# Decoding the 16 chosen routes in one 128x512 pass instead of two 128x256 passes, in an f32 two-block network on one core

## The chip, the cores and the metric

One core of one Trainium2 chip runs the whole program in one launch. The metric is the device time in microseconds (us); lower is better. The kernel before was timed in three runs, and one further execution of it was profiled.

## What is computed

The inputs are f32. A first block (norm, four mixers, projection, MLP) works on 256 tokens of width 1024. A second block has two layers over 272 tokens (16 meta tokens and the 256). Each layer ends in a product-key lookup of experts, `peer`, and that is where the change lies. Cut to it:

```python
PEER_HEADS, PEER_N_KEYS, PEER_TOPK = 8, 128, 16
def peer(h, w_query, sub_keys, u, v):          # u, v: (128 * 128, 1024) per layer
    q = einsum('btd,dq->btq', hx, w_query).reshape(B, T, 8, 2, 128)
    s = einsum('bthpc,hpnc->bthpn', q, sub_keys)            # 128 scores in each of 2 halves
    top_s, top_i = lax.top_k(s, 16)
    cand_s = (top_s[..., 0, :, None] + top_s[..., 1, None, :])      # 256 sums
    cand_i = (top_i[..., 0, :, None] * 128 + top_i[..., 1, None, :])
    best_s, best_pos = lax.top_k(cand_s, 16)
    expert = jnp.take_along_axis(cand_i, best_pos, axis=-1)
    gate = jax.nn.softmax(best_s, axis=-1)
    act = gelu(einsum('btd,bthkd->bthk', hx, u[expert]))
    return einsum('bthk,bthkd->btd', gate * act, v[expert])
```

So each token picks 8 x 16 experts, and for each of them a row of `u` and a row of `v` (4 KB each) is read from HBM.

## The kernel before, in words

The pairs of token and head are worked off in 33 **units** (`UNITS`) of 128 partitions: 32 tokens by 4 heads, and one unit with the 16 meta tokens by 8 heads. Seventeen units belong to layer 0 and sixteen to layer 1. Two neighbouring units share a group of 32 tokens. A unit has 16 **slots**, one per chosen expert; slot k needs one gathered 128x1024 f32 tile (512 KB) of `u` and one of `v`.

Five queues share the work, each strictly in the order in which the program was written:

- **GpSimd** (`peer_gpsimd`, L496 to L518) issues 528 gathers of `u` and 528 of `v`, both at L505, in turn: `u` of slot i, then `v` of slot i-22. Before a gather it waits until its ring buffer is free (7 buffers for `u`, freed by the dot product; 6 for `v`, freed by TensorE), and before the first `u` gather of a unit until VectorE has written that unit's expert numbers (`experts_ready`).
- **VectorE** (`peer_vector`, L602 to L625) takes the slots of unit s in four quarters. A quarter is four dot products of a gathered `u` tile with the token rows, which lie in PSUM (L568); then, in the first quarter, the weights of the unit before (`weights_of`, L577 to L585), in the second, the addition of a finished group to the residual (`add_group`, L598); then one of the four **stages of a route** for unit s+2 (`route`, L438 to L483). Some routes around the change of layer are placed by a table (`LATE`, L485), two stages at once.
- **TensorE** (`peer_tensor`, L642) multiplies the weights with the `v` tiles (L551) and lays the token rows of the next group into PSUM (`unit_rows`, L531 and L534). In between it computes the queries, and the attention and projections of layer 1 (L691, L760 to L787).
- **ScalarE** copies scores out of PSUM (L372) and computes exponentials and gelu (L633, L640).
- **SyncE** loads the dense weights (L1572) and stores the output.

The route of a unit, in stages: stages 0 and 1 find the top 16 of the 128 scores of either half (L449 to L453); stage 2 adds them to 256 sums and finds their top 16 (L461 to L465, then L449 to L453 again); **stage 3 is the decode**. It turns the 16 positions, each 0 to 255, into expert numbers: high and low four bits (L471, L472), made float (L473); then for either half a 16x16 one-hot matrix by comparison with 0..15 (L476), times the half's 16 indices (L478), summed along each row (L479); and last the two sums added into `expert` (L482), which signals `experts_ready`. `done` puts a drain behind each instruction of this sequence (L446). Two routes are worked before the first slot (L606 to L608); the other 31 lie in the loop.

Under L476 to L479, `w0`, `w1` and `w2` are the three 128x256 parts of the tile `work`: `w0` and `w1` hold the one-hot matrices of the two halves.

Of the kernel before, what the change touches and what calls it, by code (L numbers as in the profile page):

```python
# [8 lines left out]
ALU = mybir.AluOpType  # L9
ACT = mybir.ActivationFunctionType  # L10
X = mybir.AxisListType.X

P = 128
# [16 lines left out]
PH, KEYS, TOPK = 8, 128, 16  # L30
# [23 lines left out]
def program(nc, x, pre_mix_g, w_in, conf_dw_w, conf_dw_b, conf_gn_g, conf_gn_b, sconv_w, lru_conv_w,  # L54
# [4 lines left out]
    with ctx:  # L59
        def sb(name, shape, dt=F32):  # L60
            return ctx.enter_context(nc.sbuf_tensor(name, shape, dt))
# [3 lines left out]
        def S(name):  # L65

            if name not in named:
                named[name] = nc.alloc_semaphore(name=name)
                count[name] = 0
            return named[name]  # L70
# [39 lines left out]
        work = sb("work", [P, 3, 256])  # L110
# [3 lines left out]
        half_f = sb("half_f", [P, 2, TOPK])  # L114
        best = sb("best", [P, DEEP, TOPK])
        best_at = sb("best_at", [P, TOPK], U32)
        pos_f = sb("pos_f", [P, 2, TOPK])
        picked = sb("picked", [P, 2, TOPK])
# [6 lines left out]
        iota16 = sb("iota16", [P, TOPK])  # L125
# [164 lines left out]
        def slots_done(engine, name, n):  # L290

            layer = 0 if n <= SPLIT else 1
            engine.wait_ge(S(f"{name}{layer}"), n - SPLIT * layer)
# [132 lines left out]
        def score_slot(u):  # L426

            return u if u < L0_UNITS else 9 + (u - L0_UNITS) % 8

        def scores_ready(dve, u):  # L430

            if u < L0_UNITS:
                dve.wait_ge(S("ffn0_scores_out"), SCORE_ORDER.index(u) + 1)
            else:
                _, t, _, half = UNITS[u]
                dve.wait_ge(S("f_scores_out"), 2 * t + half + 1)

        def route(dve, u, stage):  # L438

            v = nc.vector  # L440
            at = u % DEEP
            w0, w1, w2 = (work[:, i, :] for i in range(3))
            square = [P, TOPK, TOPK]

            def done(instruction):
                dve.drain()  # L446

            def top16(values, index, source, rest):
                done(v.max(values[:, 0:8], source))  # L449
                done(v.max_index(index[:, 0:8], values[:, 0:8], source))  # L450
                done(v.match_replace(rest, values[:, 0:8], source, MASKED))
                done(v.max(values[:, 8:16], rest))  # L452
                done(v.max_index(index[:, 8:16], values[:, 8:16], rest))  # L453

            if stage < 2:
                if stage == 0:
                    scores_ready(dve, u)
                part = slice(P * stage, P * (stage + 1))
                top16(half_v[:, stage, :], half_i[:, stage, :], scores[:, score_slot(u), part], w1[:, part])
            if stage == 2:  # L460
                v.tensor_scalar(half_f[:, 0, :], half_i[:, 0, :], float(KEYS), float(UNITS[u][0] * EXPERTS),  # L461
                                ALU.mult, ALU.add)
                v.tensor_copy(half_f[:, 1, :], half_i[:, 1, :])
                sums = w2.rearrange("p (i j) -> p i j", i=TOPK)
                done(v.tensor_tensor(sums, half_v[:, 0, :].unsqueeze(2).broadcast_to(square),  # L465
                                     half_v[:, 1, :].unsqueeze(1).broadcast_to(square), ALU.add))
                top16(best[:, at, :], best_at[:], w2, w0)
            if stage == 3:
                v.tensor_scalar(neg_best[:, at:at + 1], best[:, at, 0:1], -1.0, None, ALU.mult)\
                    .then_inc(S("best_ready"), 1)  # L470
                v.tensor_scalar(ints[:, 0, :], best_at[:].bitcast(I32), 4, None, ALU.logical_shift_right)  # L471
                done(v.tensor_scalar(ints[:, 1, :], best_at[:].bitcast(I32), TOPK - 1, None, ALU.bitwise_and))  # L472
                done(v.tensor_copy(pos_f[:], ints[:]))  # L473
                for p, w in enumerate((w0, w1)):
                    onehot = w.rearrange("p (i j) -> p i j", i=TOPK)
                    done(v.tensor_tensor(onehot, pos_f[:, p, :].unsqueeze(2).broadcast_to(square),  # L476
                                         iota16[:].unsqueeze(1).broadcast_to(square), ALU.is_equal))
                    done(v.tensor_tensor(onehot, onehot, half_f[:, p, :].unsqueeze(1).broadcast_to(square), ALU.mult))  # L478
                    done(v.tensor_reduce(picked[:, p, :], onehot, X, ALU.add))  # L479
                if u >= DEEP:  # L480
                    slots_done(dve, "v_used", TOPK * (u - DEEP + 1))
                done(v.tensor_tensor(expert[:, at, :], picked[:, 0, :], picked[:, 1, :], ALU.add)  # L482
                     .then_inc(S("experts_ready"), 1))  # L483
# [5 lines left out]
        def routes_at(dve, s, j):  # L489

            late = {u for u, _ in LATE.values()}
            u, stages = LATE.get((s, j), (s + 2, (j,) if s + 2 < len(UNITS) and s + 2 not in late else ()))
            for stage in stages:
                route(dve, u, stage)
# [107 lines left out]
        def peer_vector(dve):  # L602

            v = nc.vector
            units = len(UNITS)
            for u in range(2):  # L606
                for stage in range(4):
                    route(dve, u, stage)  # L608
            for s in range(units):
                for j in range(4):  # L610
                    dots_of(dve, s, range(4 * j, 4 * j + 4))
                    if j == 0 and s >= 1:
                        weights_of(dve, s - 1)
                    if j == 1 and s >= 2 and closes_group(s - 2):
                        add_group(dve, s - 2)
                    routes_at(dve, s, j)
                    if (s, j) == (PH - 2, 3):
                        dve.wait_ge(S("ffn0_scores_done"), L0_UNITS)
                        v.tensor_copy(meta_spread.rearrange("p k (h t) -> p k h t", h=PH),
                                      hnt[:, :, 0:META].unsqueeze(2).broadcast_to([P, KD, PH, META]))\  # L620
                            .then_inc(S("meta_spread"), 1)
                    for t in range(NT):
                        attend_dve(dve, t, 4 * s + j - ATTEND[t])
            weights_of(dve, units - 1)
            add_group(dve, units - 1)  # L625
# [1061 lines left out]
```

## Time and profile before

| what | value |
|---|---|
| three timed runs, median (lowest to highest) | 2005.23 us (2003.51 to 2007.88) |
| the profiled execution, its own time | 2004.27 us |
| span of that execution in the profile | 2002.5 us |
| PE busy | 1477.6 us (74%) |
| VectorE (DVE) busy | 1187.2 us (59%) |
| GpSimd (POOL) busy | 1025.1 us (51%) |
| ScalarE (ACT) busy | 279.0 us (14%) |
| moved by DMA | 669.93 MB |

The span runs from the first to the last instruction of the profiled execution; its own time is 1.8 us longer. Busy time counts an engine's instructions, not its waits. The gathers run from 458.6 us of the span to its end; what comes before is the first block, the pooling layer and the first queries.

### The profile page before, as it was taken

How to read it: one execution, taken by the hardware profiler on the slowest of the kernel's cores; microseconds unless marked ns; L12 is line 12 of the kernel's file. 1: busy time of each engine (PE TensorE's matmuls, PEld its weight loads, DVE VectorE, ACT ScalarE, POOL GpSimd, SP SyncE). 2: the span in 40 equal slices, each digit the busy share in tenths (PEclk: the TensorE clock that was granted, in tenths of full speed). 3: DMA queues.
4: the chain of work that ended last, by engine and by line, in shares of the span. 5: the costliest groups of instructions: out<-in, count | busy, mean ns of one | idle time of the engine just before them, and what ended most of it. 6: DMA issues, size and time to landing. Idle time of an engine off the chain costs nothing.

```text
span 2002.5 us, 19164 instructions
## 1 busy us (share of the span) xinstructions
PE 1477.6 (74%) x6422; PEld 588.6 (29%) x6422; DVE 1187.2 (59%) x2799; ACT 279.0 (14%) x539; POOL 1025.1 (51%) x1099
## 2 busy tenths in 40 slices
PE   6979999784667556668888885687797866656666
PEld 5736666474233110102223222022232210101100
DVE  3641000258787756787669636976786587777752
ACT  2141111211001100001212111012321110010000
POOL 2000000004777766676556655774565677677675
PEclk9988999887688866768996998689988976677668
DMA  9113346106999999999999999999989999999998
GB/s 330 62 75 137 132 162 266 59 22 216 381 409 409 409 409 410 406 409 384 409 403 346 410 409 387 410 408 409 397 325 409 410 410 409 399 410 409 397 400 328
DMA packets 189387, 669.93 MB, mean 335 GB/s; under 512 B 19806, under 2 KB 20960, under 8 KB 188016
## 3 DMA queue, kind: packets, MB, share of 16 engines
q0 software_dynamic: 152064, 553.72, 70.4%
q1 hardware_dynamic: 37232, 115.09, 15.1%
q8 instruction: 46, 0.75, 0.2%
q14 instruction: 45, 0.37, 0.0%
HBM read 667.68 MB, written 1.05 MB: 334 GB/s over the span
## 4 chain that ended last, share of the span: by engine, by line
DMA 30%; POOL 14%; PE 14%; DVE 13%; issue 7%; DVEq 2%; ACT 1%; POOLq 0%; ACTq 0%
DMA big<-in_peer_v,expert 21%; POOL big L505 14%; DMA big<-in_peer_u,expert 9%; DVE big L568 8%; PE ps L551 4%; PE ps L691 3%; PE ps L534 2%; PE ps L334 2%; DVEq L446 2%; PE ps L785 1%; DVE residual L598 0%; PE ps L787 0%; PE ps L1657 0%; DVE half_v L452 0%; DVE diag L585 0%
## 5 line engine op out<-in xcount | busy, mean ns | idle before, releaser
L551 PE MATMUL ps<-big,diag 128*32 128x512 f32 (+1 forms) x2112 | 710.4, 792 | 438.8 <-DMA big<-in_peer_v,expert 403.1
L568 DVE CUSTOM_DVE_ANT_0 big<-big,ps 128x1024 f32<-128x1024 f32 x528 | 625.4, 1218 | 332.4 <-DMA big<-in_peer_u,expert 229.4
L505 POOL DMA_INDIRECT big<-in_peer_u,expert x528 | 501.6, 950 | 319.2 <-issue 133.8
L505 POOL DMA_INDIRECT big<-in_peer_v,expert x528 | 506.8, 960 | 249.3 <-PE ps L551 132.5
L551 PEld LDWEIGHTS ps<-big,diag 128*32 128x32 f32 (+1 forms) x2112 | 83.5, 121 | 972.3 <-DMA big<-in_peer_v,expert 848.0
L691 PE MATMUL ps<-big 128*128 128x512 f32 x384 | 195.4, 632 | 1.0 <-ACT big L880 1.0
L1585 POOL MEMSET big<- 128x128 f32 x3 | 0.5, 202 | 373.9 <-POOLq L1449 373.9
L230 DVE RECIPROCAL stats<-stats 128x1 f32<-128x1 f32 (+1 forms) x17 | 2.8, 162 | 252.0 <-ACT stats L224 251.5
L1505 PE MATMUL ps<-ua,big 128*128 128x256 f32 x512 | 116.3, 382 | 0.0
L1516 PE MATMUL ps<-big,sc 128*128 128x512 f32 x256 | 114.4, 592 | 0.0
L1505 PEld LDWEIGHTS ps<-ua,big 128*128 128x128 f32 x512 | 98.3, 192 | 25.4 <-issue 13.2
L691 PEld LDWEIGHTS ps<-big 128*128 128x128 f32 x384 | 66.9, 194 | 127.8 <-issue 125.9
L640 ACT ACTIVATE dots<-dots 128x16 f32<-128x16 f32 x33 | 7.1, 216 | 593.3 <-DVE dots L568 593.2
L334 PEld LDWEIGHTS ps<-big 128*128 128x128 f32 x512 | 71.1, 217 | 16.9 <-issue 15.8
L334 PE MATMUL ps<-big 128*128 128x144 f32 (+1 forms) x512 | 74.8, 311 | 0.8 <-DVE big L317 0.8
L1374 PE MATMUL ps<-sc,big 128*128 128x256 f32 x288 | 64.2, 385 | 3.5 <-DVE sc L1234 3.5
L598 DVE TENSOR_TENSOR residual<-residual,ps 32x512 f32<-32x512 f32 (+1 forms) x68 | 46.5, 683 | 31.2 <-PE ps L551 28.8
L1516 PEld LDWEIGHTS ps<-big,sc 128*128 128x128 f32 x256 | 48.6, 190 | 49.3 <-issue 47.8
L1374 PEld LDWEIGHTS ps<-sc,big 128*128 128x128 f32 x288 | 55.4, 193 | 11.9 <-DVE sc L1234 3.7
L534 PE MATMUL ps<-ident,big 128*32 128x128 f32 x1024 | 56.0, 341 | 0.0
L534 PEld LDWEIGHTS ps<-ident,big 128*32 128x32 f32 x1024 | 44.7, 134 | 13.8 <-issue 10.6
L640 ACT ACT_TABLE_LOAD x33 | 42.3, 1283 | 28.8 <-DVE dots L568 28.4
(293 smaller groups left out, 1201.6 us busy)
## 6 DMA issues: line engine op xcount, KB each, us to landing
big<-in_mlp_w SPq DMA_DIRECT2D x16, 2048.0 KB, 7.8
big<-in_w_kv SPq DMA_DIRECT2D x32, 512.0 KB, 6.9
big<-in_peer_wq SPq DMA_DIRECT2D x32, 512.0 KB, 6.8
big<-in_w_in SPq DMA_DIRECT2D x5, 2048.0 KB, 17.6
big<-in_peer_u,expert POOLq DMA_INDIRECT x528, 10.3
big<-in_peer_v,expert POOLq DMA_INDIRECT x528, 10.3
big<-in_peer_wq SPq DMA_DIRECT2D x1, 8192.0 KB, 27.2
big<-in_w_q SPq DMA_DIRECT2D x16, 512.0 KB, 6.9
```

The costliest lines, as they stand in the source:

```text
L334: last = nc.tensor.matmul(bank(4 + hp % 2)[:, 0:cols], wq_peer[:, k, P * hp:P * (hp + 1)], hnt[:, k, at:at + cols], start=(k == 0), stop=( ...
L446: dve.drain()
L505: nc.gpsimd.indirect_dma_start(out=ring[n % len(ring)], out_offset=None, in_=rows[name], in_offset=bass.IndirectOffsetOnAxis(ap=expert[:, ...
L534: last = nc.tensor.matmul(to[TOK * j:TOK * (j + 1), :], hnt[:, k, at:at + TOK], ident[:], start=True, stop=True)
L551: last = nc.tensor.matmul(acc[r:r + tokens, :], placed(u, tokens)[:, k, :], ring_v[n % len(ring_v)][:, BANK * half:BANK * (half + 1)], sta ...
L568: nc.vector.tensor_tensor_reduce(out=slot, in0=slot, in1=rows_x, scale=1.0, scalar=0.0, op0=ALU.mult, op1=ALU.add, accum_out=dots[:, u % 2 ...
L598: last = v.tensor_tensor(to, to, bank(group % 2)[r:r + tokens, :], ALU.add)
L640: a.activation(dots[:, s % 2, :], dots[:, s % 2, :], ACT.Gelu).then_inc(S("gelu_done"), 1)
L691: last = m.matmul(bank(b + half), src, w[:, BANK * half:BANK * (half + 1)], start=(k == 0), stop=(k == KD - 1))
L1374: last = m.matmul(bank(b)[:, T * c:T * (c + 1)], win[chunk][:, k, P * (at + c):P * (at + c + 1)], ht[:, k, :], start=(k == 0), stop=(k == ...
L1505: last = m.matmul(bank(4 + q % FT)[:, 0:T], w1b[b][:, k, P * (q % FT):P * (q % FT + 1)], h2t[:, k, :], start=(k == 0), stop=(k == KD - 1))
L1516: last = m.matmul(bank(2 * t + half), act2[:, q % FT, P * t:P * (t + 1)], w2b[b][:, q % FT, BANK * half:BANK * (half + 1)], start=False, s ...
```

## The change

Stage 3 of a route no longer loops over the two halves. `work[:, 0:2, :]`, 512 contiguous columns that hold both one-hot matrices, is seen as 32 rows of 16, and each of the three operations works on all of it at once.

```diff
-                for p, w in enumerate((w0, w1)):
-                    onehot = w.rearrange("p (i j) -> p i j", i=TOPK)
-                    done(v.tensor_tensor(onehot, pos_f[:, p, :].unsqueeze(2).broadcast_to(square),
-                                         iota16[:].unsqueeze(1).broadcast_to(square), ALU.is_equal))
-                    done(v.tensor_tensor(onehot, onehot, half_f[:, p, :].unsqueeze(1).broadcast_to(square), ALU.mult))
-                    done(v.tensor_reduce(picked[:, p, :], onehot, X, ALU.add))
+                both = [P, 2 * TOPK, TOPK]
+                flat = work[:, 0:2, :].rearrange("p w (i j) -> p (w i) j", i=TOPK)
+                halves = work[:, 0:2, :].rearrange("p w (i j) -> p w i j", i=TOPK)
+                done(v.tensor_tensor(flat, pos_f[:, :, :].rearrange("p w i -> p (w i)").unsqueeze(2).broadcast_to(both),
+                                     iota16[:].unsqueeze(1).broadcast_to(both), ALU.is_equal))
+                done(v.tensor_tensor(halves, halves, half_f[:, :, :].unsqueeze(2).broadcast_to([P, 2, TOPK, TOPK]), ALU.mult))
+                done(v.tensor_reduce(picked[:, :, :].rearrange("p w i -> p (w i)"), flat, X, ALU.add))
```

The lines behind it move down by one (L568 is L569, L585 is L586). On VectorE the program has 2350 rows before and 2251 now, 99 fewer, three for each of the 33 units; no other engine's order changes.

VectorE's order before, at the decode that stands behind the last four dot products of unit 0 (it decodes unit 2; `ISA` is the dot product, `expert` the tile that the gathers read):

```order
L568 ISA dots 128x1
L469 TENSOR_SCALAR neg_best<-best 128x1
L471 TENSOR_SCALAR ints<-best_at 128x16
L472 TENSOR_SCALAR ints<-best_at 128x16
L473 CAST pos_f<-ints 128x32
L476 TENSOR_TENSOR work<-pos_f,iota 128x256
L478 TENSOR_TENSOR work<-work,half_f 128x256
L479 TENSOR_REDUCE picked<-work 128x16
L476 TENSOR_TENSOR work<-pos_f,iota 128x256
L478 TENSOR_TENSOR work<-work,half_f 128x256
L479 TENSOR_REDUCE picked<-work 128x16
L482 TENSOR_TENSOR expert<-picked 128x16
```

The same place now:

```order
L569 ISA dots 128x1
L469 TENSOR_SCALAR neg_best<-best 128x1
L471 TENSOR_SCALAR ints<-best_at 128x16
L472 TENSOR_SCALAR ints<-best_at 128x16
L473 CAST pos_f<-ints 128x32
L477 TENSOR_TENSOR work<-pos_f,iota 128x512
L479 TENSOR_TENSOR work<-work,half_f 128x512
L480 TENSOR_REDUCE picked<-work 128x32
L483 TENSOR_TENSOR expert<-picked 128x16
L569 ISA big,dots<-big,ps 128x1024
```

Six instructions have become three of twice the width, and nothing has changed its place.

## Rows read from the trace of the kernel before

**Rows 1.** The page: the span, and what the DMA engines moved in 40 slices.
```profile
span 2002.5 us, 19164 instructions
...
GB/s 330 62 75 137 132 162 266 59 22 216 381 409 409 409 409 410 406 409 384 409 403 346 410 409 387 410 408 409 397 325 409 410 410 409 399 410 409 397 400 328
```

**Rows 2.** Busy time by stretch: stretch, length, engines (instructions), PE clock, DMA share, GB/s.
```profile
600.00:700.00 100.00, 67.02 (x428) 28.80 (x428) 74.72 (x183) 13.38 (x26) 74.40 (x79) 0.83 1.03 409
...
473.00:521.00 48.00, 9.60 (x29) 2.54 (x28) 44.75 (x111) 2.64 (x7) 28.56 (x30) 0.54 0.84 291
1050.00:1100.00 50.00, 39.09 (x165) 14.75 (x166) 46.00 (x117) 13.22 (x39) 32.08 (x34) 0.62 0.95 347
1260.00:1300.00 40.00, 25.69 (x64) 2.86 (x64) 35.98 (x102) 1.90 (x4) 29.45 (x32) 0.67 1.03 410
1436.00:1492.00 56.00, 46.12 (x286) 22.31 (x285) 49.23 (x113) 17.19 (x37) 34.10 (x34) 0.82 0.89 323
1600.00:1620.00 20.00, 11.28 (x98) 3.84 (x96) 17.43 (x42) 2.39 (x4) 14.22 (x15) 0.83 1.03 409
```

**Rows 3.** The timeline of VectorE and GpSimd where the gathers begin: start, length, instruction.
```profile
461.43 0.29 DVE L449 MAX8 half_v<-sc 128x8 f32<-128x128 f32 x1 [3.78 <-ACT sc L372]
...
473.21 1.22 DVE L568 CUSTOM_DVE_ANT_0 big<-big,ps 128x1024 f32<-128x1024 f32 x1 [0.22 <-issue]
...
474.71 0.93 POOL L505 DMA_INDIRECT big<-in_peer_u,expert  x1 [7.53 <-DVE dots L568]
...
521.52 1.22 DVE L568 CUSTOM_DVE_ANT_0 big<-big,ps 128x1024 f32<-128x1024 f32 x1 [0.56 <-DMA big<-in_peer_u,expert]
```

**Rows 4.** VectorE's timeline at one decode, that of unit 2.
```profile
499.73 0.42 DVE L476 TENSOR_TENSOR work<-pos_f,iota 128x256 f32<-128x256 f32 x1
500.22 0.43 DVE L478 TENSOR_TENSOR work<-work,half_f 128x256 f32<-128x256 f32 x1
500.72 0.42 DVE L479 TENSOR_REDUCE picked<-work 128x16 f32<-128x256 f32 x1
501.22 0.42 DVE L476 TENSOR_TENSOR work<-pos_f,iota 128x256 f32<-128x256 f32 x1
...
502.71 0.17 DVE L482 TENSOR_TENSOR expert<-picked 128x16 uint32<-128x16 f32 x1
```

**Rows 5.** VectorE's groups by form: busy us, mean ns of one, idle before.
```profile
L479 DVE TENSOR_REDUCE picked<-work 128x16 f32<-128x256 f32 x66 | 27.7, 419 | 5.6 <-issue 0.9
L585 DVE TENSOR_TENSOR diag<-weight,sel 128x512 f32<-128x512 f32 x32 | 22.1, 692 | 2.4
...
L1036 DVE TENSOR_TENSOR big<-big,head_sums 128x1024 f32<-128x1024 f32 x4 | 4.9, 1226 | 0.2
L1021 DVE TENSOR_REDUCE head_sums<-big 128x16 f32<-128x1024 f32 x4 | 4.9, 1215 | 24.5 <-ACT big L880 19.6 <-ACT big L888 4.9
```

**Rows 6.** The page: the chain that ended last, by engine.
```profile
DMA 30%; POOL 14%; PE 14%; DVE 13%; issue 7%; DVEq 2%; ACT 1%; POOLq 0%; ACTq 0%
```

**Rows 7.** The chain in order of time: start, us, what.
```profile
469.84 0.42 DVE work L476
...
1075.23 1.87 PE ps L551 x8
...
1606.92 0.42 DVE work L476
```

**Rows 8.** The timeline of all engines where a gather issue is stretched.
```profile
508.13 0.69 DVE L585 TENSOR_TENSOR diag<-weight,sel 128x512 f32<-128x512 f32 x1
508.24 1.39 POOL L505 DMA_INDIRECT big<-in_peer_v,expert  x1 [0.30 <-issue]
...
577.12 0.42 DVE L478 TENSOR_TENSOR work<-work,half_f 128x256 f32<-128x256 f32 x1
577.24 1.12 POOL L505 DMA_INDIRECT big<-in_peer_v,expert  x1 [0.31 <-issue]
...
1886.42 1.19 POOL L505 DMA_INDIRECT big<-in_peer_v,expert  x1 [0.30 <-issue]
```

## The prediction

> **What bounds the kernel now.** I read the page first, for what the DMA engines move over time [rows 1]. From the twelfth slice on (slices are 50 us) the rate stands at 409 or 410 GB/s in most slices, and in none above: that is the ceiling of this traffic. At 512 KB and 409 GB/s a gather needs 1.28 us. The stage of the gathers, from 458.6 us to the end, is three quarters of the span, and over most of it the memory sets the pace, not an engine: between 600 and 700 us VectorE is busy for 74.72 us of 100, GpSimd for 74.40, and the rate is 409 [rows 2]. Time saved on VectorE there only lets it wait longer for the next tile.
>
> Then I looked for stretches in which the rate is below 409 while VectorE never pauses. There are three [rows 2]. At 473 to 521 us it is busy for 44.75 us of 48 and the rate is 291: the DMA engines lose (409 - 291) / 409 of 48 us, 13.8 us. At 1050 to 1100 us they lose 7.6 us (347 GB/s), and at 1436 to 1492 us 11.8 us (323 GB/s). At 1260 to 1300 and at 1600 to 1620 us VectorE is just as full, but the rate is 410 and 409.
>
> The start shows why the first one is VectorE's [rows 3]. The first seven `u` gathers go out while VectorE still works on the route of unit 1; the eighth has to wait 7.53 us for the first dot product, which starts at 473.21 us because the route ended there. From then on VectorE has no pause until 521.52 us, where it first waits for a tile.
>
> **What one decode costs.** Six instructions follow each other at 0.49 to 0.50 us: 499.73 to 502.71 is 2.98 us from the first comparison to the sum into `expert` [rows 4]. An instruction takes 0.42 us, and the drain behind it adds about 0.075 us.
>
> The new comparison and product are 128x512 with two f32 inputs in SBUF. The nearest row is L585, the same operation at that size, also with repeated rows: 0.692 us [rows 5]. The new sum is a reduction of 512 columns to 32. No row has it; L479 (256 columns) takes 0.419 us and L1021 (1024) takes 1.215 us, and the straight line between them gives 0.684 us. With 0.075 us each that is 0.767 + 0.767 + 0.759 = 2.29 us. **A decode gets 0.69 us shorter**, and 33 of them are 22.8 us of VectorE's time. All three drains that go are in this; nothing is added on another engine.
>
> The bounds: if a wide instruction cost no more than a narrow one, a decode would save three steps, 1.49 us. If it cost as much as the 1024-column rows (1.226 us for a product, L1036, and 1.215 us [rows 5]), it would take 3.89 us and lose 0.91 us. I take 0.69, by L585, which differs from the new operations in nothing that I can see.
>
> **What of it is on the path.**
> - *Decode of unit 0*, before the first gather: `expert` is ready 0.69 us sooner and seven gathers start sooner. But VectorE then waits anyhow: it stood 3.78 us before the next route until ScalarE had copied the scores [rows 3], and will stand 4.5. The eighth gather hangs on VectorE. Worth nothing.
> - *Decodes of units 1 and 2*, at 469.84 and 499.73 us [rows 4, 7]: both lie in the stretch without a pause that starves the DMA engines. Each moves the first dot products, or the following ones, and with them every gather behind, 0.69 us forward: 2 x 0.69 = 1.38 us. From 521 us on the memory has the same bytes to move, from an earlier start.
> - *1050 to 1100 us*: one decode lies there too, but the chain runs over TensorE, where attention's products stand ahead of the `v` slots (L551 x8 at 1075.23, repeated about every 7 us) [rows 7]. VectorE has the next link done before it is asked for. Worth nothing.
> - *1436 to 1492 us*: two decodes, both on the chain (which visits seven decodes in all, the first at 469.84 us, the last at 1606.92 us [rows 7]). The DMA engines lose time there, so both count: 2 x 0.69 = 1.38 us.
> - *Two decodes between 1260 and 1300 us and the last at 1606.92 us*: on the chain, yet the rate is 410 and 409 [rows 2]. The chain names who came last, but the tiles stood in a full queue: hidden.
> - *The other 24*: behind them VectorE waits for a tile or for TensorE's token rows. That is the cover; if the gathers ever came faster than 1.28 us apiece, each would cost its 0.69 us again.
>
> Gain so far: 2.76 us.
>
> **What it costs on GpSimd.** There is a coupling in the trace. A gather's issue takes 0.93 us [rows 3], but 1.39 us if it begins 0.11 us after L585 has begun, and 1.12 us if it begins 0.12 us after an L478 [rows 8]. In each case it ends as if its work had stood still until the VectorE instruction was over. I counted 24 issues stretched so by L476 and L478, the first at 577.24 us and the last at 1886.42 us, 4.0 us together, 0.17 us each. A wide instruction can hold an issue for longer: the time that an issue loses grows with the square of the length, 2 x 0.69 squared against 4 x 0.42 squared, 1.35 times. So 4.0 us become 5.4, and of the 1.4 us more, GpSimd's 14% of the chain [rows 6] let 0.2 us through.
>
> The Trainium skill speaks on this in "SBUF — State Buffer", section "Who interferes with whom": a `tensor_tensor` with both inputs in SBUF holds up only GpSimd's reads, and the generation of descriptors is inferred to need the write side, so gathers would not notice it. By that rule the cost is 0 and the gain 2.76 us. The stretched issues here say otherwise, and I go by them.
>
> **The sum.** -2.76 + 0.2 = -2.5 us (-0.13%). Against the profiled execution's own 2004.27 us that is 2001.8 us. The median of the three runs is 1.0 us above it, at 2005.23 us, so I forecast a median of **2002.7 us**. The three runs lie 4.4 us apart; what a measurement can tell from no change is about 0.2%, 4.0 us, so I expect **no difference that can be measured**.
>
> **The rivals.**
> 1. *The chain is right as it stands*: all seven decodes on it count, 7 x 0.69 = 4.8 us, 2000.4 us. For it: the chain passes through all seven. Against: in three of them the DMA engines run at their ceiling. Chance 0.17. Its far end, that every decode counts (22.8 us, 1982.4 us), asks that VectorE bounds the whole stage, against 74.72 us of 100 [rows 2]; 0.04.
> 2. *Slower: the longer instructions hold back the gathers.* An issue that begins with a wide instruction loses up to 0.69 - 0.12 = 0.57 us. Gathers follow each other at no less than about 1.24 us (0.93 us and the 0.3 us before it), so at most about one per decode is caught in full: 33 x 0.57 = 18.8 us, less the 4.0 us of now, is 14.8 us, and with the gain 12.0 us slower, 2017.2 us. It decides from the point where more than 2.76 us of it, five issues caught in full, fall where GpSimd paces the DMA engines. For it: stretched issues are in the trace, and some of their starts repeat to the hundredth of a us, so they may be caught every time and not at random. Against: GpSimd is idle for a quarter of 600 to 700 us [rows 2], and stands in waits for buffers. Chance 0.11. The same page of the skill, same section, calls the shared pair of ports an exclusive lock that is held for the whole instruction, which speaks for this rival where the lock is the one met here.
> 3. *The first gain is taken back.* At each new group VectorE waits until TensorE, which stands behind `v` tiles, has laid down the rows; if that is set by something that doesn't move, the 1.38 us of the start end there. Then the time is 2004.1 us, and 2005.4 us if 1436 to 1492 us gives nothing either. Chance 0.08.
> 4. *The change doesn't do what it says*: a repeated operand over two levels runs below one column per cycle. At the upper bound, 0.91 us lost on each of the four decodes that count, 3.6 us: 2008.9 us. Chance 0.04.
>
> **How the numbers follow.** My forecast has 0.56. Faster by over 0.2%: rival 1 with 0.21, and 0.03 from forecasts in which a wide instruction is cheaper than I take it (four times 1.49 us is 6.0 us): 0.24. Slower by over 0.2%: 0.09 of rival 2 and 0.03 of rival 4: 0.12. Within 0.2%: 0.64. The range goes from 1999.2 us (four decodes at the lower bound of the price, which also holds the seven at 0.69 us) to 2006.8 us (rival 3, and the mild end of rival 2, with the runs' scatter); beyond it lie the far ends of rivals 1 and 2 and most of rival 4.
>
> **What would show it.** L477 and L479 at 0.69 us and L480 at 0.68 us, 33 times each, and 2.3 us from the comparison to `expert`; VectorE's busy time down by 33 x (2.53 - 2.07), about 15 us; its wait for gathered tiles and for rows up by about as much; the first dot product 0.7 us sooner than 473.21; the first wait for a tile after it about 1.4 us sooner than 521.52; the rate in mid-stage at 409 as before. It would be wrong if the rate's dips elsewhere filled up (rival 1), or if issues of 1.4 us and more stood at the decodes and dips of the rate behind them (rival 2).

## The result, and the profile after

| | median (lowest to highest) | runs |
|---|---|---|
| before | 2006.07 us (2003.51 to 2009.05) | 6 |
| changed | 1994.97 us (1994.14 to 1997.2) | 6 |

The ratio is 0.9945, with a 95% interval of 0.9934 to 0.9956: 11.1 us or 0.55% faster. In a second session it was 0.9937 (0.9921 to 0.9953). The forecast was 2.5 us; the measured time lies below the range.

The page of the changed kernel, as [rows 1], with VectorE's row:

```profile
span 1992.4 us, 18966 instructions
...
PE 1480.2 (74%) x6422; PEld 589.7 (30%) x6422; DVE 1171.5 (59%) x2700; ACT 279.1 (14%) x539; POOL 1025.0 (51%) x1099
...
GB/s 332 58 80 135 130 163 256 75 22 207 383 409 409 409 409 410 396 410 409 409 406 372 410 409 393 410 409 409 404 337 409 410 409 409 406 410 408 391 404 326
```

VectorE is busy 15.7 us less. The ceiling is the same 409 to 410 GB/s, but several dips are shallower: 384, 403 and 346 have become 409, 406 and 372, and 397 and 325 have become 404 and 337. One is deeper: 406 has become 396.

Its groups by form, which answer to [rows 5] (busy us, mean ns, idle before), and the timeline of the decode that answers to [rows 4]:

```profile
L479 DVE TENSOR_TENSOR work<-work,half_f 128x512 f32<-128x512 f32 x33 | 23.0, 696 | 2.4
L477 DVE TENSOR_TENSOR work<-pos_f,iota 128x512 f32<-128x512 f32 x33 | 22.8, 692 | 2.5
L480 DVE TENSOR_REDUCE picked<-work 128x32 f32<-128x512 f32 x33 | 22.6, 685 | 2.4
```

```profile
498.90 0.69 DVE L477 TENSOR_TENSOR work<-pos_f,iota 128x512 f32<-128x512 f32 x1
...
501.19 0.17 DVE L483 TENSOR_TENSOR expert<-picked 128x16 uint32<-128x16 f32 x1
```

498.90 to 501.19 is 2.29 us where it was 2.98. The prices of the instructions were right within 0.005 us.

**Where the time went.** I took the stretch of each unit, from its first dot product to the next unit's, and worked out how long the DMA engines would have stood still at 410 GB/s. Over the 32 units that have a next one that is 46.3 us before and 36.9 us after, 9.4 us less; the stretch of the last unit lost 10.0 and 10.3 us. The first dot product starts 0.8 us sooner, at 472.38 against 473.21 us. Together that is 9.9 of the 10.1 us between the two spans; the 669.9 MB and the highest rate are the same. Four units make most of it in this pair of profiles: 11, 13, 14 and 21. Busy time by stretch for 11, 13 and 21, columns as in [rows 2], first before, then after:

```profile
929.96:979.21 49.25, 45.48 (x135) 12.99 (x136) 32.22 (x77) 6.71 (x9) 29.05 (x30) 0.96 0.98 384
1043.36:1089.21 45.85, 33.06 (x150) 12.46 (x151) 41.83 (x106) 10.75 (x31) 29.53 (x31) 0.68 0.96 363
1445.99:1489.96 43.97, 38.50 (x190) 18.06 (x190) 38.53 (x91) 10.65 (x27) 26.06 (x27) 0.77 0.85 299
```

```profile
924.91:976.72 51.81, 44.30 (x138) 12.38 (x137) 32.09 (x74) 6.71 (x9) 28.87 (x31) 1.00 1.03 409
1039.51:1083.83 44.32, 34.71 (x154) 12.08 (x154) 41.23 (x104) 12.19 (x35) 30.16 (x31) 0.73 1.00 384
1436.91:1479.13 42.22, 36.75 (x186) 17.27 (x186) 37.99 (x88) 10.67 (x27) 25.32 (x26) 0.80 0.88 317
```

In unit 11 the time lost fell from 3.2 to 0.2 us, in 13 from 5.3 to 2.8, in 14 from 3.2 to 2.2, in 21 from 11.9 to 9.5.

One pair of profiles doesn't prove that the change did this in each of these places. The other profiles of this record, worked out in the same way, scatter: unit 21 lost 12.9 us in a second profile of the changed kernel, and 9.9 us in the kernel with swapped halves, which does the work of before. What does go with the decode's time in all of them is the start. Units 0 and 1 together lost 13.6 to 14.1 us in the seven profiles in which these decodes take as long as before, 12.9 to 13.2 us in the four profiles in which they take 0.69 us less, and 14.5 and 14.7 us in the two in which they take 0.69 us more.

In 13 and 14 attention of the first tile runs. TensorE's timeline in that stretch, first before, then after:

```profile
1053.58 0.38 PE L770 MATMUL ps<-ident,big 128*16 128x128 f32 x1 [3.84 <-DVE big L1061]
1063.68 0.38 PE L770 MATMUL ps<-ident,big 128*16 128x128 f32 x1 [2.86 <-DVE big L1061]
```

```profile
1070.85 0.38 PE L771 MATMUL ps<-ident,big 128*16 128x128 f32 x1 [0.66 <-DVE big L1062]
```

Before, TensorE twice stood for about 3 us because VectorE, with dot products and the first stage of a route ahead of it in its queue, had not yet written attention's weights. The `v` slots stand behind that wait on TensorE. That their buffers then come free later, and the DMA engines run dry for it, is my reading of the order.

The chain before runs through VectorE here too. Some of its pieces (start, us, what):

```profile
1043.36 1.22 DVE big L568
...
1048.09 0.43 issue
...
1063.20 0.43 DVE big L1061
1063.68 0.38 PE ps L770
```

From 1043.36 to 1063.63 us its links are VectorE's. But no decode is among them: the last one ahead ends at 1034 us, and VectorE then waits 9.12 us for the rows from TensorE (L534); the next starts at 1082.10 us. So a shorter decode cannot have shortened the two waits by its own time. After the change TensorE reached the first of them 9.8 us behind the unit's first dot product and not 6.4, since it had waited for `v` tiles, and found it done.

The 3.2 us of unit 11 are of yet another kind. TensorE's timeline has this row for the new group's transposes, before and then after:

```profile
926.19 3.63 PE L534 MATMUL ps<-ident,big 128*32 128x128 f32 x56
```

```profile
922.85 1.92 PE L535 MATMUL ps<-ident,big 128*32 128x128 f32 x56
```

And the busy time of the 5 us around it, columns as in [rows 2], before and then after:

```profile
925.00:930.00 5.00, 5.00 (x67) 3.38 (x60) 0.36 (x3) 0.00 (x0) 0.88 (x1) 0.50 1.03 410
```

```profile
920.00:925.00 5.00, 3.50 (x73) 2.44 (x70) 3.09 (x6) 0.08 (x1) 3.13 (x4) 1.00 1.03 411
```

The granted clock was 0.50 (1.2 GHz) in the one case and 1.00 (2.4 GHz) in the other. In the 5 us ahead of the first stretch TensorE had been busy for 1.99 us, in short pieces, and the granted clock there was 0.86. The profile of the kernel with swapped halves, with the same work as before, loses only 0.2 us in unit 11, so the change is not needed to win this piece.

### The profile page after: what moved, and what is told of

Its sections match the earlier page's. It is cut to its first block, busy times and chain, and to the rows that moved or that the text cites. A ratio compares the mean times of both kernels' runs of the same rounds, so it can differ in the third digit from the quotient of the medians.

```text
span 1992.4 us, 18966 instructions
## 1 busy us (share of the span) xinstructions
PE 1480.2 (74%) x6422; PEld 589.7 (30%) x6422; DVE 1171.5 (59%) x2700; ACT 279.1 (14%) x539; POOL 1025.0 (51%) x1099
## 4 chain that ended last, share of the span: by engine, by line
DMA 32%; PE 15%; DVE 13%; POOL 12%; issue 6%; DVEq 2%; ACT 1%; POOLq 0%; ACTq 0%
DMA big<-in_peer_v,expert 25%; POOL big L506 12%; DVE big L569 8%; DMA big<-in_peer_u,expert 7%; PE ps L552 5%; PE ps L692 3%; PE ps L535 2%; DVEq L446 2%; PE ps L334 2%; PE ps L786 1%; PE ps L788 1%; PE ps L1658 0%; DVE residual L599 0%; PE ps L696 0%; DVE half_v L452 0%
## 5 line engine op out<-in xcount | busy, mean ns | idle before, releaser
L569 DVE CUSTOM_DVE_ANT_0 big<-big,ps 128x1024 f32<-128x1024 f32 x528 | 625.8, 1218 | 345.5 <-DMA big<-in_peer_u,expert 241.5
L1506 PEld LDWEIGHTS ps<-ua,big 128*128 128x128 f32 x512 | 98.3, 192 | 25.4 <-issue 13.2
L1375 PEld LDWEIGHTS ps<-sc,big 128*128 128x128 f32 x288 | 55.5, 193 | 11.9 <-DVE sc L1235 3.7
```

Of the source, the lines that this page charges most:

```text
L569: nc.vector.tensor_tensor_reduce(out=slot, in0=slot, in1=rows_x, scale=1.0, scalar=0.0, op0=ALU.mult, op1=ALU.add, accum_out=dots[:, u % 2 ...
L1375: last = m.matmul(bank(b)[:, T * c:T * (c + 1)], win[chunk][:, k, P * (at + c):P * (at + c + 1)], ht[:, k, :], start=(k == 0), stop=(k == ...
L1506: last = m.matmul(bank(4 + q % FT)[:, 0:T], w1b[b][:, k, P * (q % FT):P * (q % FT + 1)], h2t[:, k, :], start=(k == 0), stop=(k == KD - 1))
```

## The experiments

All ratios are against the kernel before, run in the same session; microseconds gained or lost are the ratio's distance from 1, times 2006 us, unless the text says otherwise. The differences of the medians are within 1.4 us of them, but for fused (7.6 against 11.0 us); the recorded expectations use the medians' 4.7 us for wide_padded. "Time" is what a decode takes more (+) or less (-) on VectorE than in the kernel before, from the groups' mean times.

| kernel | time per decode | ratio (95% interval) | median |
|---|---|---|---|
| swapped | 0 | 0.9997 (0.9988 to 1.0006) | 2005.62 |
| shift_43 | 0 | 0.9978 (0.9968 to 0.9989) | 2002.19 |
| shift_86 | 0 | 0.9977 (0.9966 to 0.9988) | 2001.58 |
| wide_padded | 0 | 0.9974 (0.9964 to 0.9984) | 2001.86 |
| narrow_padded | +0.69 us | 1.0003 (0.9994 to 1.0012) | 2006.82 |
| wide_twice_padded | +0.69 us | 1.0005 (0.9995 to 1.0015) | 2006.93 |
| one_wide | -0.23 us | 0.9968 (0.9956 to 0.9980) | 2000.44 |
| short_again | -0.45 us | 0.9964 (0.9951 to 0.9978) | 1996.95 |
| changed, first | -0.69 us | 0.9945 (0.9934 to 0.9956) | 1994.97 |
| wide_again, the same kernel | -0.69 us | 0.9937 (0.9921 to 0.9953) | 1993.54 |
| wide_shift_43 | -0.69 us | 0.9956 (0.9939 to 0.9973) | 1997.13 |
| fused | -0.94 us | 0.9945 (0.9927 to 0.9964) | 1998.6 |
| w_0_10 | -0.69 us in 11 of 33 | 0.9965 (0.9954 to 0.9977) | 1998.72 |
| w_11_21 | -0.69 us in 11 of 33 | 0.9982 (0.9973 to 0.9991) | 2001.85 |
| w_22_32 | -0.69 us in 11 of 33 | 0.9989 (0.9981 to 0.9998) | 2003.95 |

### Where along the program

```diff
+                if u <= 10:
...
+                else:
...
```

The first branch holds the wide decode, the second the narrow one of before; the other two kernels have `11 <= u <= 21` and `u >= 22` in the condition.

> Only the decodes of units 0 to 10 are wide, the other 22 stay as before. Theory A (VectorE's saved time returns place by place, where the DMA engines starve; read off the idle time of the DMA engines unit by unit in the two traces): 1 to 2 us faster than before, the gain of units 1 and 2. Theory B (the saving moves the whole stage against TensorE's granted clock and the ring of buffers, so that gains don't add up by place): any value, and the three partial kernels don't add up to the 11.1 us of the full change. Theory C (every decode's 0.69 us counts for half, wherever it is): 3.7 us faster.

> Only the decodes of units 11 to 21 are wide. Theory A: 7 to 8 us faster (the DMA engines idle 7.4 us less over units 11 to 16 in the trace of the full change, while attention of the first tile runs). Theory B: not near 7.5 us, and the sum of the three is not 11.1 us. Theory C: 3.7 us faster.

> Only the decodes of units 22 to 32 are wide. Theory A: 1 to 3 us faster (2.3 us in unit 21, where the decode of unit 23 lies, and little behind it). Theory B: no sum of the three to 11.1 us. Theory C: 3.7 us faster.

The gains were 7.0, 3.6 and 2.2 us, 12.8 together. That is near the whole, which speaks against theory B as a denial of any sum, but the shares are not those of theory A: the first eleven give most, although in the trace of the full change little is won before unit 11. They are not those of theory C either. In the profile of w_0_10 the DMA engines lose 3.2 and 2.2 us in units 13 and 14, nearly as little as in the full change, though the decodes there are narrow. Something other than the time of those decodes works at a distance.

### The same time in another form

```diff
+        unused = sb("unused", [P, 2 * TOPK])
...
                 done(v.tensor_reduce(picked[:, :, :].rearrange("p w i -> p (w i)"), flat, X, ALU.add))
+                done(v.tensor_reduce(unused[:, 0:28], work[:, 0:2, :].rearrange("p w (i j) -> p (w i) j", i=TOPK)[:, 0:28, :], X, ALU.add))
```

> The full change, and behind each decode one more reduction of 448 columns of the one-hot tile into an unused tile, with its drain: about 0.69 us, so that a decode takes as long as before. If only VectorE's time matters, it equals the kernel before within 0.1% (2 us). If the fewer and wider instructions matter by themselves (GpSimd's issues held up differently), it differs: faster if the held issues were the cause, slower if wide instructions hold more.

The extra reduction took 0.620 us, a decode as long as before, and the kernel was still 5.2 us faster (4.7 us by the medians). So VectorE's time is not all. The next four asked what is:

```diff
-                for p, w in enumerate((w0, w1)):
+                for p, w in ((1, w1), (0, w0)):
```

> The kernel before with the two halves decoded in the other order: the same instructions, as many and as long. If only VectorE's time and what it holds up decide, it equals the kernel before, within 0.1% (2 us). If the time hangs on small chances of alignment or of where code lies, it may differ by some us, as the padded wide kernel did (4.7 us faster at an equal decode time).

Equal to before (0.9997).

The narrow padded kernel has the reduction of 448 columns behind the old loop.

> The kernel before with the same extra reduction of 448 columns as in the padded wide kernel, 0.69 us more per decode. Theory of VectorE's time, at the rate of the change (11.1 us for 33 times 0.69 us): 10 to 12 us slower than before. At the rate between the padded wide kernel and the full change (6.9 us for the same 0.69 us): 6 to 8 us slower. If the memory hid it as the prediction had it: 2 to 3 us slower.

0.6 us slower: 22.8 us more on VectorE seemed to cost nothing, as the prediction's view would have it. The later kernels show that this reading is too simple.

The third joins only the comparison (L476) into one wide instruction.

> Only the comparison is one 128x512 instruction; product and sum stay two narrow ones each. Saves 0.23 us per decode. By VectorE's time: 2.3 us (at 6.9 us per 0.69) to 3.7 us (at 11.1 us per 0.69) faster. If the width or the number of instructions has an effect of its own (the 4.7 us of the padded kernel, for three joined pairs), about 1.6 us more.

6.4 us faster (5.7 us by the medians), for 0.23 us per decode: far more than time accounts for.

```diff
+                grid = work[:, 0:2, :].rearrange("p a b -> p (a b)").rearrange("p (i w j) -> p w i j", w=2, j=TOPK)
...
-                done(v.tensor_tensor(expert[:, at, :], picked[:, 0, :], picked[:, 1, :], ALU.add)
...
+                    done(v.tensor_reduce(expert[:, at, :], work[:, 0:2, :].rearrange("p a b -> p (a b)")
+                                         .rearrange("p (i n) -> p i n", n=2 * TOPK), X, ALU.add)
+                         .then_inc(S("experts_ready"), 1))
```

Comparison and product, left out here, write `grid`.

> The full change, with the one-hot tile laid out so that both halves of a route lie side by side: one reduction of 32 columns per route writes the expert number, and the addition behind it goes. Saves another 0.25 us per decode. By VectorE's time: another 2.5 to 4 us faster than the full change, 1991 to 1993 us. If the memory hid it: within 1 us of the full change.

0.9945, like the change; not shown better, though 0.25 us less per decode. Its six runs fall apart, into two at 1990.4 us and four from 1997.8 to 2001.7 us.

### Where the instructions lie

The kernels with an equal time differ in one more thing: how many VectorE instructions stand ahead of a given one. VectorE's timeline shows short pauses of 0.2 to 0.5 us before which nothing is waited for. One of them in VectorE's timeline of the kernel before, and then the same one in the kernel with swapped halves:

```profile
1048.52 0.28 DVE L579 SCALAR_TENSOR_TENSOR weight<-dots,gate_sum,gate 128x16 f32<-128x16 f32 x1 [0.43 <-issue]
```

```profile
1049.85 0.29 DVE L579 SCALAR_TENSOR_TENSOR weight<-dots,gate_sum,gate 128x16 f32<-128x16 f32 x1 [0.43 <-issue]
```

They stand at the same lines in both, 17 of 0.2 us and more after 440 us, 6.8 us together. Counted by VectorE's records in the trace, those of its sequencer included, 16 of the 17 lie a multiple of 128 records apart (one of them a record late), and 12 other such places show none that long. The 17th, ahead of the first dot product, is there in every kernel. Behind each of the 16 begins, 2.0 to 3.4 us later, one 8 KB packet of the queue for instructions. For the pause at 1048.52 us that is the packet at 1051.8 us; the DMA queues from 1051 to 1053 us (packets, MB, share):

```profile
q14 instruction: 1, 0.01, 1.0%
```

So the pauses go with the loading of the program, and with other numbers of instructions they stand elsewhere. In shift_43, for example:

```profile
1071.83 0.09 DVE L453 MATCH_VALUE_LOAD best_at<-best,work 128x8 f32 x1 [0.42 <-issue]
```

So I moved the stream and left the work alone, with 43 (86) drains in the first block, where VectorE waits over 200 us:

```diff
+                for _ in range(43):
+                    dve.drain()
                 dve.wait_ge(S("gain1_loaded"), 16)
```

> The kernel before with 43 drains more on VectorE, early, where it waits over 200 us for the first block's MLP: the work is the same, but every later VectorE instruction lies 43 places further on in its instruction stream. The traces show short pauses of VectorE (0.2 to 0.5 us, 'issue') at fixed places of the stream: the same lines in the kernel before and in the one with swapped halves, others wherever the number of instructions differs. Theory F (where these pauses fall decides): the time moves, by up to 5 us either way. Theory S (the form of the decode decides): equal to the kernel before within 2 us.

> The changed kernel with the same 43 early drains. Theory F: its gain changes by some us, in the direction of the kernel before if its places were lucky. Theory S: equal to the changed kernel within 2 us.

> The kernel before with 86 early drains. If the kernel before lies in an unlucky place: faster than before again, 0.997 to 0.999. If 43 met a lucky one: 1.000. On a chip with the lower memory rate: 1.0 in either case.

The kernel before became 4.4 us faster by 43 drains (0.9978), and 4.6 us by 86 (0.9977). The gain lies in the gathers' stage: in the profiles the first dot product comes 1.0 and 1.8 us later than in the kernel before. The changed kernel went from 0.9937 to 0.9956 in the same session, which the intervals don't tell from no change. The kernel before had met an unlucky place, and so had the one with swapped halves, which has as many instructions. Against 0.9978 and 0.9977, the padded wide kernel's 0.9974 is nothing strange any more: equal time, equal result.

The same view accounts for the three kernels above that are wide in eleven units each, though no run was made to test it there. A third of the 6 us that the change gives by time (below) is 2 us. In w_22_32 everything ahead of unit 22's decode lies where it did before, and 2.2 us were measured. In w_0_10 nearly everything lies elsewhere, 2 and 4.8 us make 6.8, and 7.0 were measured. w_11_21 lies between, at 3.6. What would have tested the place most sharply is missing: 128 drains, after which, by the count above, the pauses should be back at the old instructions.

> The changed kernel once more, beside the others on the same chip: 1994 to 1996 us, 0.994 to 0.996 of before, if the first measurement holds; the spread of its runs is the measure for the others.

> The changed kernel with two extra reductions of 448 columns per decode: 0.69 us per decode longer than the kernel before, as the narrow padded kernel is (which was 0.6 us slower than before, no difference to be told). If time counts at the rate between the changed and the once padded kernel (6 to 7 us per 0.69 us): 2007 to 2009 us, slower than before. If the wide form has a gain of its own that time doesn't take back: 2001 to 2003 us, below the narrow padded kernel of equal length.

The second padded wide kernel and the narrow padded one, both at +0.69 us, agree (1.0005 and 1.0003). So the wide form shows no gain of its own that more time doesn't take back.

### VectorE's time at an equal number of instructions

```diff
+                rows, times = (2 * TOPK, 2) if long else (1, 1)
+                done(v.tensor_reduce(unused[:, 0:rows * times].rearrange("p (i n) -> p i n", n=times),
+                                     work[:, 0:2, :].rearrange("p w (i j) -> p (w i) j", i=TOPK)[:, 0:rows, :]
+                                     .unsqueeze(2).broadcast_to([P, rows, times, TOPK]), X, ALU.add))
```

> The changed kernel with one short extra reduction (16 columns into an unused tile) and its drain behind each decode, about 0.2 us: the base for the three that follow, which have the same number of instructions. By VectorE's time at 6 us per 0.69 us and decode: 1.5 to 2.5 us slower than the changed kernel, 1995 to 1998 us.

> As the short one, but for the decodes of units 0 to 10 the extra reduction reads 1024 columns (some 1.0 us longer). The prediction's place theory: only units 1 and 2 count, 2 us slower than the short one. Evenly spread at 25% of the time: 11 us more on VectorE, 3 us slower.

> As the short one, with the long reduction in the decodes of units 11 to 21, where attention of the first tile runs on VectorE too. Place theory from the idle time of the DMA engines: 3 to 5 us slower than the short one. The prediction had them hidden: 0 us. Evenly spread: 3 us.

> As the short one, with the long reduction in the decodes of units 22 to 32, attention of the second tile and the last units. The prediction had two of them on the path: 2 us slower than the short one. Evenly spread: 3 us.

These four ran on a chip on which the kernel before took 2110.94 us. Their ratios were 0.9992 (0.9974 to 1.0009), 1.0007 (0.9993 to 1.0020), 1.0001 (0.9985 to 1.0017) and 0.9994 (0.9981 to 1.0006): no difference to be told, although a long reduction took 1.220 us and a short one 0.170. The page of short_all, as in [rows 1]:

```profile
GB/s 314 90 41 130 159 159 239 30 91 300 357 359 353 366 411 386 346 388 353 409 408 349 404 409 358 362 361 410 336 356 409 409 348 385 355 356 356 359 373 329
```

In many slices the rate is 348 to 362 GB/s instead of 409. Whether the chip is slower or something beside the kernel took its share, no run shows. The intervals, 2.6 to 3.8 us to either side, exclude neither that 11.6 us more on VectorE (11 long reductions) are hidden nor that they cost the 3 us expected. The question by stretch stays open, and the base ran once more on a chip with 409 GB/s:

> The changed kernel with one short extra reduction and drain per decode, the same instructions in the same places as in the once padded kernel, 0.45 us less per decode. If VectorE's time counts at 409 GB/s (6 us per 0.69 us between the padded and the changed kernel): 4 us faster than the padded kernel, 0.995 to 0.996 of before, 1996 to 1998 us. If the difference between the padded and the changed kernel was one of places in the stream: 0.997, as padded. On a chip with the lower memory rate: 0.999 to 1.0.

0.9964, against 0.9974 of the once padded kernel with the same instructions in the same places. The direction is that of VectorE's time; the two intervals overlap, and I had expected 0.995 to 0.996.

## Why the prediction was wrong

Two terms of the sum failed. The gain by VectorE's time was put at 2.76 us less 0.2, with the time of all but four decodes hidden or worth nothing, and about 6 us came. The smaller number of instructions was given no term at all, and where the instructions lie brought close to 5 us more. Step by step:

**What a decode costs**: right. 0.692, 0.696 and 0.685 us against 0.692, 0.692 and 0.684; 0.69 us saved.

**Decodes of units 0, 1 and 2**: right. From the first dot product to the expert number of unit 2 it took 28.81 us instead of 29.50, 0.69 us less, and over all profiles units 0 and 1 lose less or more with the decode's time, as shown above. The times by the clock prove less: the first dot product came 0.83 us sooner in the first profile of the changed kernel, but 1.7 us later in the second (474.92 us). One announced sign did not come: the first wait for a tile was at 527.32 us and not 1.4 us sooner than 521.52.

**GpSimd's issues held up**: right in kind, nearly right in size, and small. Comparisons and products held up 24 issues for 4.1 us before and 23 for 5.9 us after (5.4 forecast). GpSimd's two groups took 1008.4 us in both. Rival 2 falls. The stretched issues stand against the rule of the Trainium skill quoted in the prediction ("SBUF — State Buffer", section "Who interferes with whom") here too: a `tensor_tensor` with both inputs in SBUF holds back the issue of a gather.

**"Worth nothing" for 1050 to 1100 us**: the reason was wrong. The sentence "VectorE has the next link done before it is asked for" was not read from a row. The list of who waited for whom had one against it:

```profile
PE ps L770 <- DVE big L1061: 7.9, 3, 3.8
```

The chain itself had VectorE's links up to 1063.63 us; I had looked at a later part, around 1075.23 us, which runs over TensorE. After the change the list reads 1.2 us, 2 times, and units 13 and 14 lost 3.5 us less. What that step cost the forecast is not shown, though. No decode lies ahead of the waits, w_0_10 with narrow decodes there loses 5.4 us in 13 and 14, nearly as little as the changed kernel (5.0), and the wait is a sign and not a measure: shift_86 has 11.0 us of it in its profile and is no slower than shift_43 with 1.9, and wide_twice_padded has 1.6 us, none of them in unit 13, and loses 5.2 us there.

**1436 to 1492 us**: two decodes, counted for 1.38 us. The profiles can't tell: unit 21 loses 9.3 to 15.0 us in them, without order by the decode's time. Nor does VectorE work there without a pause, as the prediction says of the three stretches: at 1470.83 us it had waited 2.76 us for ScalarE.

**The sum of the gain, with "hidden" for the other 24**: the term that was sized wrongly. Take the kernels at 0 us away from the unlucky place, 0.9974 to 0.9978. At +0.69 us the ratio is 1.0003 to 1.0005, 0.0028 or 5.6 us more; at -0.69 us it is 0.9937 to 0.9956, on average 0.0030 or 6.1 us less. So of 22.8 us on VectorE about 25% to 27% reach the end, on both sides, where the prediction had 2.5 us, 11%. By the intervals of the ratios a sixth to a third is as compatible. The line through these points also fits kernels that it was not drawn from: it gives 0.9967, 0.9957 and 0.9937 for one_wide, short_again and fused, and 0.9968, 0.9964 and 0.9945 were measured, all with the line inside their intervals. Where the 6 us arise is open. They are near rival 1's 4.8 us for its seven decodes on the chain; an even share of every decode fits as well, and no run tells the two apart. The sign that the prediction had named for rival 1, dips of the rate that fill up, was there.

**What no step had**: the place of the instructions. The sum gave 99 fewer instructions no term of their own, and that is 4.4 to 5.2 us of the 11. About 6.1 us of time and about 4.8 us of place make 10.9 of the measured 11.1; the place is luck, since another count of instructions in the kernel before would have left it out. The chance of 0.24 for faster held both too low: an error of this kind had no place in the range.

What stays open: how the place does it. The pauses of 0.2 us and more sum to 6.8 us before, 5.8 and 5.4 us in shift_43 and shift_86, and 4.1 us in the once padded kernel. The 1.0 to 2.7 us between them are less than what is gained. That a pause in attention costs more than itself, through the waits above, is tempting: the one of 0.43 us at 1048.52 us lies on the chain, and w_22_32 has it too and loses 6.5 us in unit 13. But w_11_21 loses 6.3 us there and shift_43 only 1.1, the first with no pause in that unit and the second with one, and the once padded kernel loses 5.1 us and is as fast as the shifted ones.

## What to carry to other kernels

Before a share of a change is called hidden under a full queue, look at each stretch in which the queue is not full, and there read the whole chain and every engine's waits on the engine that gets faster. Then ask whether the changed instructions themselves lie ahead of these waits. A result of half a per cent in a stage of tightly coupled queues should be checked against a kernel whose work is the same and whose instructions lie elsewhere: a few drains where the engine is idle are enough, and here they gave 40% of the change's gain. And a unit or stretch that improves in one profile should be looked up in a second profile of the same kernel before the change gets the credit.

## What I had not expected of the hardware

- 43 or 86 drains of an idle VectorE, hundreds of us ahead of the stage, changed the time by 0.22% and 0.23%, 4.4 and 4.6 us.
- VectorE pauses for 0.2 to 0.5 us at places a multiple of 128 of its records apart, 16 times after 440 us in the kernel before, and 2.0 to 3.4 us behind each an 8 KB packet of its program is loaded. The same remainder of the count holds in the other profiles with 409 GB/s.
- In one session the gathers got 348 to 362 GB/s in many 50 us slices, in the others 409; the same kernel took 2111 us there and 2006 us elsewhere, and no difference between kernels could be told.
- Single executions of one kernel lie up to 12 us apart (fused, 1990.4 to 2001.7 us): a profile of one of them shows losses that another doesn't, such as the 3.2 us of unit 11.
